# A down projection in seven half-size products over its whole contraction, with block sums added in DRAM

## The chip, the cores and the metric

The kernel runs on one core of one Trainium2 chip. The metric is the device time of one execution, in microseconds (us), lower is better. The core has TensorE (PE, matrix products into the eight banks of PSUM), VectorE (DVE), ScalarE (ACT), GpSimd (POOL) and SyncE (SP); in this kernel SP issues nearly all transfers.

## The reference, cut to what matters

One decoder layer over 1024 tokens of width 1024, all in float32. Everything up to the second residual is the same before and after the change; what counts here is the gated feed-forward part:

```
D_MODEL = 1024;  SEQ = 1024;  D_FF = 2816
x = x + rms_norm(mix, norm_mix_post)
h = rms_norm(x, norm_ffn_pre)
up = causal_dwconv(einsum('bsd,df->bsf', h, ffn_w_up), ffn_conv_w) + ffn_conv_b
gate, val = split(up, 2, axis=-1)
ff = einsum('bsf,fd->bsd', silu(gate) * val, ffn_w_down)      # the down projection
x = x + rms_norm(ff, norm_ffn_post)
```

Ahead of it stand an RMSNorm, the input projection `w_in`, the three mixers (pool, conv, windowed attention) and the output projection `w_o`.

## The kernel before

**How a product is made.** Every float32 operand is split into a rounded part (`hi`, ACT makes it by a copy to the short type) and the rest (`lo`, DVE makes it by subtraction), and each product is three matmuls: hi by hi, lo by hi, hi by lo (helper `product`, lines 1441 to 1443). The unit of PE's work is one matmul of 128 by 128 weights against 512 columns.

**Stages in order.** Input projection and mixers; `w_o` in eight token tiles (ACT squares, POOL computes the root in `root`, lines 563 and 566, DVE scales); the up projection; the down projection with the last norm. The up projection goes over 22 pairs of 128-channel tiles (a gate tile and a value tile). Pairs 0 to 2 are plain (`plain_step`), pairs 3 to 21 use seven products of half size instead of eight (`seventh`, 84 matmuls a pair). For those, POOL adds weight blocks (`sum_weights`, lines 595 to 602), and DVE and ACT split them (`low_entry`, `round_entry`). The gated result of a pair, silu(gate) times value, is made by DVE in `gate_value` (line 1284) in one of two SBUF buffers `yv`; SP writes it to `act_dram` (`save_act`, line 432), since it doesn't fit in SBUF. ACT may write a `yv` buffer again for pair p+2 in `keep`, once the save of pair p has landed (`act_saved`).

**The down projection.** It runs in two passes over the token halves. In each pass the eight banks hold 4 token tiles by 2 output halves, and the 22 channel tiles k run through them: for each k, one weight tile of 128 by 1024 (512 KB, into one of `RAW` = 4 buffers `wraw`) and one activation tile of 128 by 512 (256 KB, `act_in`) are loaded by SP, rounded by ACT (`down_step`), split by DVE (lines 992 and 1269), and used by PE in 24 matmuls (`down_ring`). Two split slots exist. The first two activation tiles are loaded early into `gain_a` (`act_first`). Between the passes ACT and DVE copy the eight banks to `ff`; the first four token tiles are normed and written out in the second pass. The last `TAIL` = 4 channel tiles of the second pass are kept back in buffers of their own, so that the last banks finish one by one: 2 passes x 22 x 24 = 1056 matmuls.

**What sets the order.** Each engine's program is a list in its own order, and semaphores join them; an engine that waits holds everything behind it. POOL in particular does its adds, its roots and its transfers in one list.

## Time and profile before

| what | value |
|---|---|
| time before, median of 3 runs | 1002.41 us (999.76 to 1004.15) |
| profiled execution: time, span | 1003.03 us, 1001.2 us |
| PE busy | 983.2 us (98%), 4580 matmuls |
| DVE, ACT, POOL busy | 613.3 us (61%), 407.8 us, 158.2 us |
| granted TensorE clock, mean | 0.994 |
| bytes moved | 104.90 MB, mean 105 GB/s |

The span is the profiled time from the first to the last instruction; the execution's own time holds 1.83 us more. A busy PE is not PE at its peak: its matmul records are pipelined and overlap (each is 0.39 us long, and they start 0.23 us apart), so that distances between starts are read, not lengths.

### The profile page before, as it was taken

How to read it: one execution, taken by the hardware profiler on the slowest of the kernel's cores; microseconds unless marked ns; L12 is line 12 of the kernel's file. 1: busy time of each engine (PE TensorE's matmuls, PEld its weight loads, DVE VectorE, ACT ScalarE, POOL GpSimd, SP SyncE). 2: the span in 40 equal slices, each digit the busy share in tenths (PEclk: the TensorE clock that was granted, in tenths of full speed). 3: DMA queues.
4: the chain of work that ended last, by engine and by line, in shares of the span. 5: the costliest groups of instructions: out<-in, count | busy, mean ns of one | idle time of the engine just before them, and what ended most of it. 6: DMA issues, size and time to landing. Idle time of an engine off the chain costs nothing.

```text
span 1001.2 us, 11938 instructions
## 1 busy us (share of the span) xinstructions
PE 983.2 (98%) x4580; PEld 810.0 (81%) x4580; DVE 613.3 (61%) x641; ACT 407.8 (41%) x624; POOL 158.2 (16%) x143
## 2 busy tenths in 40 slices
PE   8999999999999998999999999999999999999997
PEld 7988777777888887888888888888887888888886
DVE  4646786664555579777677677677665333344454
ACT  5525444443343335444445445445433323333342
POOL 2200000000111832332242232232200000000001
PEclk9999999999999999999999999999999999999999
DMA  6511110016223321232223223223315444455553
GB/s 221 154 49 37 43 43 22 25 61 209 85 85 104 86 84 47 80 93 86 75 79 90 84 66 102 85 64 105 105 64 191 155 139 144 157 191 197 182 175 126
DMA packets 84911, 104.90 MB, mean 105 GB/s; under 512 B 3849, under 2 KB 63489, under 8 KB 84865
## 3 DMA queue, kind: packets, MB, share of 16 engines
q1 hardware_dynamic: 84737, 104.20, 31.9%
q8 instruction: 31, 0.51, 0.2%
q14 instruction: 15, 0.12, 0.0%
q0 software_dynamic: 128, 0.07, 0.0%
HBM read 84.33 MB, written 19.92 MB: 104 GB/s over the span
## 4 chain that ended last, share of the span: by engine, by line
PE 91%; DVE 3%; DMA 2%; ACT 1%; POOL 1%; issue 1%; SPq 0%; DVEq 0%; POOLq 0%; ACTq 0%
PE ps L1441 29%; PE ps L1442 29%; PE ps L1443 29%; PE ps L1451 1%; PE ps L1549 1%; PE ps L1572 1%; DMA wraw<-in_w_in 1%; PE ps L1550 1%; PE ps L1558 1%; PE ps L1576 1%; DMA wraw<-in_w_o 1%; DMA act_in<-act_dram 0%; DVE hlo L992 0%; PE ps L1587 0%; DVE w2lo L1316 0%
## 5 line engine op out<-in xcount | busy, mean ns | idle before, releaser
L992 DVE TENSOR_TENSOR wlo<-wraw,whi 128x1024 fp32r<-128x1024 f32 x60 | 75.8, 1265 | 138.1 <-ACT whi L633 137.8
L633 ACT ACTIVATE whi<-wraw 128x1024 fp32r<-128x1024 f32 x60 | 63.4, 1058 | 173.4 <-PE ps L1443 169.3
L1441 PE MATMUL ps<-whi,ahi 128*128 128x512 f32 x320 | 124.6, 389 | 1.6 <-DVE alo L1269 1.6
L1443 PE MATMUL ps<-whi,alo 128*128 128x512 f32 x320 | 124.5, 389 | 0.0
L1442 PE MATMUL ps<-wlo,ahi 128*128 128x512 f32 x320 | 124.5, 389 | 0.0
L1441 PE MATMUL ps<-hhi,whi 128*128 128x512 f32 (+1 forms) x256 | 96.4, 376 | 2.3 <-DVE hlo L1010 2.3
L1442 PE MATMUL ps<-hlo,whi 128*128 128x512 f32 (+1 forms) x256 | 93.7, 366 | 0.0
L1443 PE MATMUL ps<-hhi,wlo 128*128 128x512 f32 (+1 forms) x256 | 93.7, 366 | 0.0
L563 POOL TENSOR_SCALAR meansq<-sumsq 128x1 f32<-128x1 f32 x28 | 7.6, 272 | 526.7 <-ACT x2b L804 241.7
L595 POOL TENSOR_TENSOR w_sums<-wraw 128x1024 f32<-128x1024 f32 x19 | 46.7, 2459 | 255.2 <-DVE h2lo L1316 103.4
L1441 PEld LDWEIGHTS ps<-whi,ahi 128*128 128x128 f32 x320 | 60.1, 188 | 14.4 <-DVE alo L1269 2.0
L1443 PEld LDWEIGHTS ps<-whi,alo 128*128 128x128 f32 x320 | 60.1, 188 | 12.6
L1442 PEld LDWEIGHTS ps<-wlo,ahi 128*128 128x128 f32 x320 | 60.1, 188 | 12.4
L1441 PE MATMUL ps<-h2hi,whi 128*128 128x512 f32 x168 | 65.5, 390 | 0.0
L1442 PE MATMUL ps<-h2lo,whi 128*128 128x512 f32 x168 | 65.4, 389 | 0.0
L1443 PE MATMUL ps<-h2hi,wlo 128*128 128x512 f32 x168 | 65.4, 389 | 0.0
L1441 PEld LDWEIGHTS ps<-hhi,whi 128*128 128x128 f32 x256 | 49.1, 192 | 10.0 <-DVE hlo L1010 2.7
L1443 PEld LDWEIGHTS ps<-hhi,wlo 128*128 128x128 f32 x256 | 49.1, 192 | 7.6
L1442 PEld LDWEIGHTS ps<-hlo,whi 128*128 128x128 f32 x256 | 49.1, 192 | 7.4 <-issue 0.5
L1441 PE MATMUL ps<-hhi,mhi 128*128 128x512 f32 x128 | 51.3, 401 | 2.2 <-DVE hlo L992 2.2
L1442 PE MATMUL ps<-hlo,mhi 128*128 128x512 f32 x128 | 50.6, 395 | 0.0
L1443 PE MATMUL ps<-hhi,mlo 128*128 128x512 f32 x128 | 50.5, 394 | 0.0
(196 smaller groups left out, 2215.8 us busy)
## 6 DMA issues: line engine op xcount, KB each, us to landing
wraw<-in_ffn_w_up SPq DMA_DIRECT2D x44, 512.0 KB, 5.1
wraw<-in_ffn_w_down SPq DMA_DIRECT2D x44, 512.0 KB, 3.4
act_dram<-yv SPq DMA_DIRECT2D x22, 512.0 KB, 2.6
act_in<-act_dram SPq DMA_DIRECT2D x42, 256.0 KB, 3.5
wraw<-in_w_in SPq DMA_DIRECT2D x14, 512.0 KB, 4.0
xin<-in_x SPq DMA_DIRECT2D x8, 512.0 KB, 4.3
wraw<-in_w_o SPq DMA_DIRECT2D x8, 512.0 KB, 3.3
xres<-in_x SPq DMA_DIRECT2D x8, 512.0 KB, 4.2
```

Of the source, the lines that this page charges most:

```text
L595: pool.tensor_tensor(w_sums[:, 0:2, :], raw[:, 0:4:3, :], raw[:, 2:3, :].broadcast_to([P, 2, HALF]), ALU.add)\
L633: act.activation(hi[:, slot, :], wraw[:, base % RAW, :], ACT.Copy)\
L992: dve.tensor_tensor(lo[:, slot, :], wraw[:, base % RAW, :], hi[:, slot, :], ALU.subtract).then_inc(w_split, 1)
L1441: pe.matmul(acc, w_hi, x_hi, start=first, stop=False, skip_group_check=looped)
L1442: pe.matmul(acc, w_hi, x_lo, start=False, stop=False, skip_group_check=looped)
L1443: return pe.matmul(acc, w_lo, x_hi, start=False, stop=last, skip_group_check=looped)
L1451: last = pe.transpose(ps[:, b + k // 4, (k % 4) * P:(k % 4 + 1) * P], rows[:, k * P:(k + 1) * P], ident)
L1549: pe.matmul(acc, q, k_hi[:, kv, keys], start=True, stop=False)
L1550: last = pe.matmul(acc, q, k_lo[:, kv, keys], start=False, stop=True)
L1558: last = pe.transpose(ps[:, 6, i * P:(i + 1) * P], prob[:, u % 2, i, :], ident)
L1572: last = pe.matmul(acc, v_tok[:, b, cols], pt_cur[:, heads, :].rearrange("p h q -> p (h q)"), start=True, stop=b == 0)
L1576: last = pe.matmul(acc, v_tok[:, b - 1, cols], pt_prev[:, heads, :].rearrange("p h q -> p (h q)"), start=False, stop=True)
```

## The change

The down projection is no longer two passes of eight blocks. The contraction (2816 channels) is cut in two halves of `HK` = 11 channel tiles (near and far), the tokens in two halves of 512, the output columns in two halves of 512. With A[channel half][token half] the activations and W[channel half][column half] the weights, seven products of 11 channel tiles each are made (the numbers are those of `DOWN_PRODUCTS`, in the order in which they run):

- 1: A11 by W11; 2: A21 by W21; 7: (A22 - A12) by s3; 5: (A11 - A12) by s1; 6: (A11 - A12 + A22) by s2; 3: A22 (negated in the split) by s4; 4: (A11 - A12 + A22 - A21) by W22,
- with s1 = W12 + W22, s3 = W11 + W12, s2 = W11 + s1, s4 = W21 + s2.

Each product has 11 steps of 12 matmuls (4 token tiles x 3): 924 matmuls. A step loads two tiles of 128 by 512 (256 KB each) side by side in one `wraw` buffer, and they are split as one 128 by 1024 tile, in one of six slots (`DOWN_RING`). The first two steps of a product run tile by tile, so do its last two (the last four of the last product), which gives ACT and DVE time to copy or add the finished banks (`copy_product`, `add_product`) before PE takes them again.

The sums are not made by an engine. The weight sums s1 to s4 are made in DRAM: POOL issues four copies of 1408 by 512 blocks (2.88 MB each), waits for them, and issues adding transfers (`accum_op`) onto them, in the stretch in which it had nothing to do (after its three memsets, ahead of the roots of the `w_o` stage); the last of them it issues after the quarter sums. The activation combinations go into `r_dram`: for pairs below 11, SP writes the blocks (five transfers of 256 KB instead of one of 512 KB), for pairs 11 to 21 POOL issues three adding transfers of 256 KB (`add_act`) between its weight sums. DVE makes the difference of the two token halves for each pair (`act_sum`, 128 by 512) in `gate_value`. ACT's rewriting of `yv` now also waits for the adding transfers (`buffer_saved`).

The core of the diff:

```
+HK = NF // 2
+DOWN_PRODUCTS = ((1, 0, True), (2, 0, False), (7, 4, True), (5, 0, True), (6, 0, False),
+                 (3, 0, False), (4, 4, False))
+STEPS = 7 * HK
+DOWN_RING = 6
+LEAD = 2
...
+            def load_step(s):
+                i, k = divmod(s, HK)
+                if s < RAW:
+                    sp.wait_ge(u_split, 4 * (SEVEN - 2 + s // 2) + 4)
                 else:
+                    sp.wait_ge(d_split, s - RAW + 1)
...
+                sp.dma_start(wraw[:, raw, 0:HALF], act_src).then_inc(down_landed[raw], 16)
+                sp.dma_start(wraw[:, raw, HALF:], w_src).then_inc(down_landed[raw], 16)
...
+                if p < HK:
+                    sp.dma_start(act_dram[rows, 0:HALF], yv[:, j, 0:HALF]).then_inc(act_saved[j], 16)
+                    sp.dma_start(r_dram[7][rows, :], yv[:, j, HALF:]).then_inc(act_saved[j], 16)
+                    sp.wait_ge(sum_ready, p + 1)
+                    for i in (5, 6, 4):
+                        sp.dma_start(r_dram[i][rows, :], act_sum).then_inc(sum_saved, 16)
...
             pool.wait_ge(ht_split, NT)
             for buf in (pool_u, sum_a, sum_b):
                 pool.memset(buf[:, 0:PAD], 0.0).then_inc(pads, 1)
+            for i, (d, k) in ((1, (1, 0)), (3, (0, 0)), (2, (0, 0)), (4, (0, 1))):
+                pool.dma_start(s_dram[i][:, :], w_down_blocks[d, k]).then_inc(w_copied, 16)
+            pool.wait_ge(w_copied, 16 * 4)
+            pool.dma_start(s_dram[1][:, :], w_down_blocks[1, 1], accum_op=ALU.add)\
+                .then_inc(w_summed, 16)
+            pool.dma_start(s_dram[3][:, :], w_down_blocks[1, 0], accum_op=ALU.add)\
+                .then_inc(w_summed, 16)
+            pool.wait_ge(w_summed, 32)
+            pool.dma_start(s_dram[2][:, :], s_dram[1][:, :], accum_op=ALU.add,
+                           max_dma_last_dim=4 * HALF).then_inc(w_summed, 16)
             for i in range(NT, 3 * NT):
                 root(i, i + 1)
...
+            def add_act(p):
...
+                pool.wait_ge(act_ready, p + 1)
+                pool.wait_ge(act_saved[k % 2], saved(k))
+                pool.wait_ge(sum_saved, 48 * (k + 1))
+                for i in (7, 6):
+                    pool.dma_start(r_dram[i][rows, :], yv[:, j, HALF:], accum_op=ALU.add)\
+                        .then_inc(act_added[j], 16)
+                pool.wait_ge(sum_ready, p + 1)
+                pool.dma_start(r_dram[4][rows, :], act_sum, accum_op=ALU.add).then_inc(sum_added, 16)
...
+                dve.wait_ge(act_ready, p + 1)
+                if p >= 1:
+                    sum_saved_of(dve, p - 1)
+                dve.tensor_tensor(act_sum, y[:, far], y[:, near],
+                                  ALU.add if p < HK else ALU.subtract).then_inc(sum_ready, 1)
...
+            for s in range(4, STEPS):
+                i, k = divmod(s, HK)
+                if k == LEAD and i - 1 in (2, 4, 5):
+                    for t in range(4):
+                        add_product(i - 1, t)
+                low_step(s)
+                if i == 6 and LEAD + 2 <= k < LEAD + 6:
+                    finish_tile(k - LEAD - 2)
...
+            for i, (_, bank, fresh) in enumerate(DOWN_PRODUCTS):
+                at_end = LEAD if i < 6 else TAIL
+                groups = [range(LEAD)] + [range(k, k + 1) for k in range(LEAD, HK - at_end)]
+                groups.append(range(HK - at_end, HK))
+                for ks in groups:
                     for t in range(4):
...
+                            if t == 0:
+                                pe.wait_ge(d_split, s + 1)
+                            hi, lo = step_place(s, False), step_place(s, True)
+                            last = product(ps[:, bank + t, :], hi[:, tok], lo[:, tok], hi[:, HALF:],
+                                           lo[:, HALF:], fresh and k == 0, k == HK - 1, True)
```

POOL's list around the three memsets, before the change:

```order
27 L574 DMA pool_mat<-in_pool_w 64x64 x3
28 L578 MEMSET pool_u 128x16 [waits ht_split]
29 L578 MEMSET sum_a 128x16
30 L578 MEMSET sum_b 128x16
31 L563 TENSOR_SCALAR meansq<-sumsq 128x1 [waits squares_summed]
32 L566 TENSOR_TENSOR rstd<-meansq,power 128x1 [waits meansq_ready]
```

The same place after it:

```order
28 L610 MEMSET pool_u 128x16 [waits ht_split]
29 L610 MEMSET sum_a 128x16
30 L610 MEMSET sum_b 128x16
31 L613 DMA s_dram<-in_ffn_w_down 1408x512 x4
32 L615 DMA s_dram<-in_ffn_w_down 1408x512 [waits down_weight_blocks_copied]
33 L617 DMA s_dram<-in_ffn_w_down 1408x512
34 L620 DMA s_dram<-s_dram 1408x512 [waits down_weight_blocks_added]
35 L595 TENSOR_SCALAR meansq<-sumsq 128x1 [waits squares_summed]
36 L598 TENSOR_TENSOR rstd<-meansq,power 128x1 [waits meansq_ready]
```

Seven transfers and two waits on transfers now stand ahead of the roots of the `w_o` stage.

DVE's list in the second pass of the down projection before (one norm of a 1024-wide tile and the splits of one channel tile after it):

```order
549 L1392 SCALAR_TENSOR_TENSOR ob<-ff,rstd,gain_a 128x1024
550 L985 REGISTER_ALU
551 L1394 ISA [waits dve_step]
552 L1395 TENSOR_TENSOR ob<-ob,x2f 128x1024 [waits x2_in0]
553 L991 REGISTER_ALU
554 L992 TENSOR_TENSOR wlo<-wraw,whi 128x1024 [waits w_rounded]
555 L1268 REGISTER_ALU
556 L1269 TENSOR_TENSOR alo<-act_in,ahi 128x512 [waits act_rounded]
```

DVE's list in the last of the seven products after (the line 1338 is one step's split, 1471 the adding of a finished bank, 1476 and 1480 the norm of one token tile):

```order
612 L1471 TENSOR_TENSOR ffb<-ps,ffb 128x512 [waits down_banks_done] x4
613 L1338 TENSOR_TENSOR w2lo<-wraw,w2hi 128x1024 [waits down_steps_rounded] x2
614 L1338 TENSOR_TENSOR dlo<-wraw,dhi 128x1024 [waits down_steps_rounded]
615 L1476 SCALAR_TENSOR_TENSOR ob<-ffb,rstd,gain_a 128x1024 [waits rstd_ready]
616 L1480 TENSOR_TENSOR ob<-ob,x2f 128x1024 [waits x2_in0,dve_step]
617 L1338 TENSOR_TENSOR dlo<-wraw,dhi 128x1024 [waits down_steps_rounded]
618 L1476 SCALAR_TENSOR_TENSOR ob<-ffb,rstd,gain_a 128x1024 [waits rstd_ready]
619 L1480 TENSOR_TENSOR ob<-ob,x2f 128x1024 [waits x2_in1,dve_step]
```

The four norms, which stood one in every four channel tiles, now stand behind four steps in a row, each of them half as long for PE.

## Rows read from the trace of the kernel before

**Rows 1.** The page: busy by engine; clock; chain; a group (busy, mean ns | idle).

```profile
PE 983.2 (98%) x4580; PEld 810.0 (81%) x4580; DVE 613.3 (61%) x641; ACT 407.8 (41%) x624; POOL 158.2 (16%) x143
...
PEclk9999999999999999999999999999999999999999
...
PE 91%; DVE 3%; DMA 2%; ACT 1%; POOL 1%; issue 1%; SPq 0%; DVEq 0%; POOLq 0%; ACTq 0%
...
L633 ACT ACTIVATE whi<-wraw 128x1024 fp32r<-128x1024 f32 x60 | 63.4, 1058 | 173.4 <-PE ps L1443 169.3
```

**Rows 2.** Timeline of PE: start, length, instruction, idle time before it with its releaser.

```profile
753.83 0.39 PE L1441 MATMUL ps<-whi,ahi 128*128 128x512 f32 x1
...
764.48 0.39 PE L1443 MATMUL ps<-whi,alo 128*128 128x512 f32 x1
766.49 0.50 PE L1441 MATMUL ps<-whi,ahi 128*128 128x512 f32 x1 [1.62 <-DVE alo L1269]
```

**Rows 3.** Timeline of DVE in the first pass, two channel tiles.

```profile
838.64 1.23 DVE L992 TENSOR_TENSOR wlo<-wraw,whi 128x1024 fp32r<-128x1024 f32 x1 [3.61 <-ACT whi L633]
...
844.08 1.23 DVE L992 TENSOR_TENSOR wlo<-wraw,whi 128x1024 fp32r<-128x1024 f32 x1 [3.61 <-ACT whi L633]
```

**Rows 4.** Timeline of POOL: its idle stretch ahead of the `w_o` stage.

```profile
34.14 2.29 POOL L574 DMA_DIRECT2D pool_mat<-in_pool_w  x4
...
39.40 0.11 POOL L578 MEMSET sum_b<- 128x16 f32 x1
237.08 0.18 POOL L563 TENSOR_SCALAR meansq<-sumsq 128x1 f32<-128x1 f32 x1 [197.57 <-ACT x2b L804]
```

**Rows 5.** DMA issues: KB each, median us to landing.

```profile
wraw<-in_ffn_w_down SPq DMA_DIRECT2D x44, 512.0 KB, 3.4
...
act_in<-act_dram SPq DMA_DIRECT2D x42, 256.0 KB, 3.5
wraw<-in_w_in SPq DMA_DIRECT2D x14, 512.0 KB, 4.0
```

**Rows 6.** Windows: busy us of each engine (x instructions), granted clock, DMA share, GB/s.

```profile
764.00:768.00 4.00, 2.38 (x11) 1.62 (x10) 2.59 (x4) 2.10 (x3) 0.00 (x0) 1.00 1.01 349
...
885.00:905.00 20.00, 20.00 (x90) 16.57 (x89) 8.90 (x9) 6.83 (x9) 0.00 (x0) 1.00 0.59 209
```

**Rows 7.** The chain in order of time, around the step from plain to seven-product pairs.

```profile
391.32 2.28 DVE r_lo L1301
```

**Rows 8.** Timelines of DVE, ACT and POOL in one pair of the steady up stage.

```profile
604.85 1.28 DVE L1264 SCALAR_TENSOR_TENSOR yv<-ps,par_a,yv 128x1022 f32<-128x1022 f32 x1
606.17 1.23 DVE L1284 SCALAR_TENSOR_TENSOR yv<-yv,yg 128x1024 f32<-128x1024 f32 x1
...
609.87 0.60 ACT L877 ACTIVATE yv<-ps 128x512 f32<-128x512 f32 x1 [2.12 <-PE ps L1443]
...
628.91 0.60 ACT L877 ACTIVATE yv<-ps 128x512 f32<-128x512 f32 x1 [2.12 <-PE ps L1443]
...
611.45 1.23 DVE L1316 TENSOR_TENSOR w2lo<-w_sums,w2hi 128x1024 fp32r<-128x1024 f32 x1 [2.92 <-ACT w2hi L864]
...
615.08 2.39 POOL L595 TENSOR_TENSOR w_sums<-wraw 128x1024 f32<-128x1024 f32 x1 [13.57 <-DVE h2lo L1316]
```

**Rows 9.** Timeline of DVE: one norm in the second pass.

```profile
884.91 1.28 DVE L1392 SCALAR_TENSOR_TENSOR ob<-ff,rstd,gain_a 128x1024 f32<-128x1024 f32 x1 [0.84 <-POOL rstd L566]
886.34 1.23 DVE L1395 TENSOR_TENSOR ob<-ob,x2f 128x1024 f32<-128x1024 f32 x1
887.61 1.23 DVE L992 TENSOR_TENSOR wlo<-wraw,whi 128x1024 fp32r<-128x1024 f32 x1
```

**Rows 10.** Timelines of ACT and DVE: the last bank.

```profile
995.31 0.60 ACT L972 ACTIVATE yg<-ps 128x512 f32<-128x512 f32 x1 [2.03 <-PE ps L1443]
...
996.03 0.69 DVE L1424 TENSOR_TENSOR ob<-ps,gain_a 128x512 f32<-128x512 f32 x1 [2.03 <-ACT yg L972]
...
997.27 1.41 DVE L1431 SCALAR_TENSOR_TENSOR ob<-ob,rstd,x2f 128x512 f32<-128x512 f32 x2 [0.55 <-POOL rstd L623]
```

More of the change, by code:

```diff
@@ L348, in build, with saved, added, buffer_saved @@
         score_view = banks(4).rearrange("p (i w j) -> p i w j", w=2, j=P)
-        NQ = 6
+        def saved(p):
+            return 16 * sum(2 if i < HK else 1 for i in range(p % 2, p + 1, 2))
+        def added(p):
+            return 32 * len(range(HK + (HK + p) % 2, p + 1, 2))
+        def buffer_saved(engine, p):
+            engine.wait_ge(act_saved[p % 2], saved(p))
+            if p >= HK:
+                engine.wait_ge(act_added[p % 2], added(p))
+        def sum_saved_of(engine, p):
+            if p < HK:
+                engine.wait_ge(sum_saved, 48 * (p + 1))
+            else:
+                engine.wait_ge(sum_added, 16 * (p + 1 - HK))
+        def step_place(s, lo):
+            at = s % DOWN_RING
+            return (((wlo if lo else whi), (w2lo if lo else w2hi), (dlo if lo else dhi))[at // 2])[:, at % 2, :]
+        def step_raw(s):
+            return (DOWN0 + s) % RAW
         def block_of(hi, i):
@@ L892, in start_value, with round_step, copy_product, square @@
                    .then_inc(yv_started, 1)
-            def round_act(raw, hi, slot):
-                act.activation(hi[:, slot, :], raw, ACT.Copy).then_inc(a_rounded, 1)
+            def round_step(s):
+                i = s // HK
+                before = s - DOWN_RING
+                if s < 2:
+                    act.wait_ge(seven_done, 7 * (SEVEN - 2) + 6 + s)
+                elif s < 4:
+                    act.wait_ge(seven_done, 7 * (SEVEN - 1) + 2 + s)
+                elif s < DOWN_RING:
+                    act.wait_ge(seven_done, 7 * SEVEN)
+                elif before % HK >= HK - LEAD:
+                    act.wait_ge(bank_done, 4 * (before // HK + 1))
+                else:
+                    act.wait_ge(step_done, (HK - LEAD) * (before // HK) + before % HK + 1)
+                act.wait_ge(down_landed[step_raw(s)], 32 * (s // RAW + 1))
+                hi, raw = step_place(s, False), wraw[:, step_raw(s), :]
+                if i == NEGATED:
+                    act.activation(hi[:, 0:HALF], raw[:, 0:HALF], ACT.Copy, scale=-1.0)
+                    act.activation(hi[:, HALF:], raw[:, HALF:], ACT.Copy).then_inc(d_rounded, 1)
+                else:
+                    act.activation(hi, raw, ACT.Copy).then_inc(d_rounded, 1)
+            def copy_product(i, t):
+                out = {0: ffb[:, t, 0:HALF], 1: ffa[:, t, 0:HALF], 3: ffa[:, t, HALF:]}[i]
+                act.wait_ge(bank_done, 4 * i + t + 1)
+                act.activation(out, ps[:, t, :], ACT.Copy).then_inc(part_copied, 1)
+            def square(src, total, seen):
+                if seen > 0:
+                    act.wait_ge(squared, 3 * NT + seen)
+                act.activation(src[1], src[0], ACT.Square, accum_out=total).then_inc(squared, 1)
             for q in x2_saved:
@@ L977, in _ @@
+            for t in range(4):
+                square((ffa[:, t, 0:HALF], yg[:, 0, 0:HALF]), half_sums[:, 2 * t:2 * t + 1], 4 + t)
+            for t in range(4):
+                act.wait_ge(bank_done, 24 + t + 1)
+                square((ps[:, 4 + t, :], yg[:, 0, 0:HALF]), half_sums[:, 2 * t + 1:2 * t + 2], 8 + t)
         @block.vector
@@ L1398, in _ @@
             dve.wait_ge(gain_out_in, 16)
-            dve.wait_ge(ff_act, 2)
-            dve.wait_ge(ff_dve, 2)
-            start = steps[0]
-            with dve.Fori(0, 4) as it:
-                steps[0] = start + it
-                for j in range(4):
-                    down_step(d1 + 2 + j, it, a1 + 2 + j)
-                    if j == 0:
-                        finish(ff[:, bass.ds(it, 1), :].rearrange("p o c -> p (o c)"),
-                               3 * NT, 3 * NT + 1 + it, 0, 16 * it + 16)
-                dve.wait_ge(out_saved[0], 16 * it + 16)
@@ L1426, in _ @@
[L1426 to L1432 removed]
+                    dve.scalar_tensor_tensor(ob[:, t, cols], ob[:, t, cols],
+                                             rstd[:, i:i + 1], x2f[:, t, cols],
@@ L1703, in _ @@
                 seventh(q, 7, 3, 0, r_hi[3], r_lo[3], v0, False)
-            def down_ring(t, k, first=False, last_k=False):
-                tok, slot = slice(t * P, (t + 1) * P), k % 2
-                for c in range(2):
-                    cols = slice(c * HALF, (c + 1) * HALF)
-                    last = product(ps[:, 2 * t + c, :], ahi[:, slot, tok], alo[:, slot, tok],
-                                   whi[:, slot, cols], wlo[:, slot, cols], first, last_k, True)
-                return last
```

414 lines of the change are left out of this document (183 added, 231 removed).

## The prediction, made before the changed kernel ran

> **What bounds the kernel now.** I read the page first. PE is busy for 98% of the span, and the chain that ended last lies on PE for 91% [rows 1]; the granted clock stands at 9 tenths or more in every slice, so nothing is to be had from the clock. Then PE's timeline at the start of the down projection, for the distance between starts, since the lengths overlap. From 753.83 to 764.48 us there are 48 matmuls, so 10.65 / 47 = 0.2266 us each [rows 2]. DVE's rows say the same from the other side: one channel tile of 24 matmuls takes 844.08 - 838.64 = 5.44 us, 0.2267 us each [rows 3], and in each DVE waits 3.61 us for ACT, which waits for PE. So in the down projection PE sets the pace and the others wait for it. There is one gap, before the activation tiles of the first pass arrive: the next start is 766.49, 2.01 us after the last, which is 1.78 us too late [rows 2]. DMA isn't the limit either: while PE ran without a gap from 885 to 905 us, 209 GB/s were moved at a share of 0.59, and in a burst 349 GB/s [rows 6].
>
> **The change, part by part.**
>
> *Products.* 1056 matmuls become 7 x 11 x 12 = 924, of the same form (128 by 128 weights, 512 columns). 132 x 0.2267 = **-29.9 us**, on the path. The order of the loops can't make a matmul shorter, and if the feed keeps up not longer.
>
> *The gap at 764.5 us.* It came from activations that could be loaded only after the last pair was saved. Now products 1 and 2 begin with the near and the far channels of the first token half; the steps up to 10 read only pairs 0 to 10, saved long before. Next late at this place would be DVE: it ends the last pair about 8 us after the up projection's last matmul (two taps each for gate and value, 1.28 us apiece, the product 1.23 [rows 8] and the new difference 0.7), while four steps, 4 x 2.72 = 10.9 us of PE work, are split beforehand. **-1.8 us.** It could come back as 0 to 2 us if step 4 is late.
>
> *Weight sums in DRAM.* Seven transfers on POOL. Their cover is the stretch from 39.40 to 237.08 us in which POOL waits 197.57 us [rows 4]. Ahead of the roots POOL waits for four copies (11.5 MB written) and two additions (5.8 MB). No row shows a transfer from DRAM to DRAM, or one that adds. From below: at 349 GB/s [rows 6] 17.3 MB take 50 us. From above: at the rate of one lone load of `w_in`, 512 KB in 4.0 us = 131 GB/s [rows 5], and twice that time for the additions, 88 + 88 = 176 us, and if the loads of `w_in` and `w_o` in the stretch (18 tiles of 512 KB, 72 us at the same rate) take their turns in full, 248 us, 50 us too many. Issuing: POOL spends 2.29 / 4 = 0.57 us on a transfer of 64 rows [rows 4]; if that goes by rows, 1408 rows are 12.6 us, six of them 75 us, beside the moving. I take **0 us**, near the lower end, since sixteen engines with a long list in front of them look like the burst and not like the lone load; the ends are 0 and +50. The w_in loads are held back by sharing, but each has four buffers' lead (over 30 us), so I give that 0 (at most +2). The fourth sum is issued after the quarter sums and is needed 57 us into the down projection: 0.
> The Trainium skill says under "Collectives: The Full Stack" (The bandwidth ceiling: the fold count and why AG ≠ RS ≠ AR) that an adding transfer reads two sources and so moves at half the speed of a copy; by that the additions cost what two copies do, an estimate that lies inside my bounds and leaves the term at 0.
> A rule against this change is in "SBUF — State Buffer" (Summary: rules for kernel authors): transfers issued by GpSimd wait for descriptors while VectorE is in one of its fast copy modes. DVE's subtraction of 128 by 1024 takes 1.23 us here [rows 3], about one element per lane and cycle of the 0.96 GHz which the skill's first page (Trainium Kernel Development and Optimization, NeuronCore Architecture) gives, so by the rule nothing would starve; no row shows such a transfer beside DVE.
>
> *Activation sums.* Per pair DVE gets one more 128 by 512 operation, 0.69 us as in [rows 10], and a wait for its own result, some 0.85 us in all. In the steady pairs DVE idles 2.92 us right behind it [rows 8]: hidden. Once it isn't: after pair 2 the chain runs through DVE (split of r at 391.32) [rows 7]: **+0.85 us** (0 to +2). POOL's three adding transfers per pair cost 3 x 0.57 to 3 x 1.15 us of issue, in a stretch of 13.57 us idle [rows 8]: hidden. ACT rewrites a `yv` buffer in `keep`, at 609.87 and 628.91 [rows 8]. The result of pair p is ready at 606.17 + 1.23 = 607.4, and the rewriting of its buffer comes one pair after the next `keep`, at 628.91: 21.5 us for issue and landing of transfers of 256 KB, of which plain ones land in 3.5 us [rows 5]. 0 us; each microsecond by which they overrun the 21.5 would cost 11 us, one per pair from 11 on.
>
> *Feeding the steps.* A step moves 512 KB in 2.72 us, 193 GB/s; 209 were carried without a gap [rows 6]. ACT (1.06 us [rows 1]) and DVE (1.23 [rows 3]) need less than 2.72 each, and four raw buffers allow 4 x 2.72 - 1.06 - 1.23 = 8.6 us per load, against 3.4 to 3.5 us [rows 5]. 0 us; if the loads bound the steps at x us each, 77 x (x - 2.72).
>
> *Six changes of product.* PE comes back to a bank 4.1 us after it left it (three other tiles of 6 matmuls), and a copy or an addition of 128 by 512 is 0.7 us. ACT and DVE take up step 2 of the next product only after the last bank: 0.7 + 1.06 + 1.23 = 3.0 us, and PE has two steps, 5.44 us. 0 us (at most +1 each).
>
> *Last product.* After its step 4, DVE does a norm of 2.70 us (884.91 to 887.61 [rows 9]) behind each of four splits of 1.15: 3.85 us for each step against PE's 2.72. Counted from the end of the sixth product, DVE has added its last bank at 0.9 us, begins the split of step 4 at 3.6 (ACT, which also squares the finished rows, is the later one there), those of steps 5 to 8 at 3.85 us each after the last (7.45, 11.3, 15.15, 19.0), and ends that of step 10 at 19.0 + 3 x 1.15 = 22.5. PE runs steps 0 to 6 until 19.04; its last four steps go tile by tile, three matmuls each, so it wants step 10 at 21.0: **+1.5 us** (0 to +3.5). DVE's four small products follow (2.4 us), and the last banks then come every 2.72 us to a DVE that needs 2.65 for each (0.69 and 1.41 and the wait for the root, 0.55 [rows 10]), and catches up little: **+0.5 us** (0 to +2). The rest of the end, from the last bank's square at 995.31 to the last row of DVE and its store [rows 10], stays.
>
> *Sum.* -29.9 - 1.8 + 0 + 0.85 + 0 + 0 + 1.5 + 0.5 = -28.85 us. The span of 1001.2 becomes 972.3, the execution 1003.03 - 28.85 = 974.2 us; it lay 0.6 us above the median, so on the median's footing 973.6. I predict **974 us**.
>
> **Rivals.**
> *POOL held by the weight sums: slower.* If the six transfers last longer than the 197.57 us, the roots of the `w_o` stage are late by the rest, and PE with them. It decides against the change from a delay of 28 us on, that is, below 17.3 MB / 226 us = 77 GB/s. At 60 GB/s they last 288 us: +90 us, 1065 us. For it: no row shows such transfers, and two waits in a list do stand there. Against it: even the pessimistic rate leaves a tie.
> *The steps are fed too slowly: same or a little slower.* Two loads of half the size per step, from blocks in DRAM with a pitch of their own; a step of 3.1 us (169 GB/s) eats the whole gain, 1003 us; 3.2 us gives 1012. Against it: 209 GB/s ran without a gap.
> *A part of the gain is lost in waits: 985 to 997 us.* The adding transfers overrun their 21.5 us by 1 or 2 us (+11 to +22), or each change of product costs 2 us (+12).
> *The change doesn't do what it says:* matmul starts 0.2267 us apart would have to grow; with the same form I see no reason.
>
> **How the numbers follow.** Forecast (970 to 985): 0.70. Part of the gain lost (985 to 997): 0.13. Fed too slowly (997 to 1015): 0.06, half of it within the band of no change. POOL held (1007 to 1100): 0.09. Matmuls slower: 0.02, slower than before. A measurement of this kernel can tell about 0.5% (5 us) from no change. Faster by more: 0.70 + 0.13 = 0.83; within: 0.04, with some of the others' edges; slower: 0.13. The range leaves out 2 in 10 at most: from 969 (without the costs of the last product, 972, and a little) to 995.
>
> **What would show it right or wrong.** Right: 924 matmuls of the down projection at 0.227 us; POOL's first root of the `w_o` stage still near 237 us; no gap of PE near 764 us; a gap of about 2 us in the last 15 us, with DVE's split of step 10 as its releaser; in the up stage ACT's `keep` never released by a transfer. Wrong: a first root after 240 us released by a DMA; gaps of PE behind `wraw` loads, at steps or at changes of product; starts further apart than 0.23 us; a longer idle time of PE near 395 us than one more microsecond.

## The result, and the profile after

The changed kernel took 972.7 us (median of 4 runs, 971.0 to 973.7) against 1001.6 us for the kernel before beside it (median of 4, 999.8 to 1004.2): a ratio of 0.9705, 95% interval 0.9689 to 0.972. The prediction was 974 us, within 969 to 995. The profiled execution took 972.8 us with a span of 971.0; the profiled span before was 1001.2, so 30.2 us are to be found. I first show where they are, then the experiments.

The page of the kernel after, answering to [rows 1] and [rows 5]: busy time by engine, the clock in 40 slices, the chain that ended last, and DMA issues with KB each and median us to landing.

```profile
PE 951.6 (98%) x4448; PEld 783.6 (81%) x4448; DVE 651.4 (67%) x688; ACT 424.9 (44%) x634; POOL 197.9 (20%) x184
...
PEclk9999999999999999899999999999999999999999
...
PE 90%; DVE 5%; DMA 3%; ACT 1%; issue 0%; SPq 0%; POOL 0%; DVEq 0%; POOLq 0%; ACTq 0%
...
s_dram<-in_ffn_w_down POOLq DMA_DIRECT2D x6, 2816.0 KB, 28.2
...
wraw<-in_w_in SPq DMA_DIRECT2D x14, 512.0 KB, 11.0
```

PE has 4580 - 4448 = 132 matmuls fewer. It still bounds the kernel, busy for 98% of the span. DVE has risen from 613.3 to 651.4 us and from 3% to 5% of the chain. The one low slice of the clock is the 17th, at 388 to 413 us.

PE's timeline after: start, length, instruction, and the idle time before it with its releaser. First the gap between the plain pairs and the first seven-product pair, then the start of the down projection, the place of the old gap [rows 2], and the last matmul.

```profile
391.12 0.39 PE L1515 MATMUL ps<-r_hi,w2lo 128*128 128x512 f32 x1
395.52 0.76 PE L1513 MATMUL ps<-r_hi,h2hi 128*128 128x512 f32 x1 [4.01 <-DVE h2lo L1397]
...
754.45 0.39 PE L1513 MATMUL ps<-whi 128*128 128x512 f32 x1
...
764.42 0.39 PE L1515 MATMUL ps<-w2hi,w2lo 128*128 128x512 f32 x1
764.65 0.39 PE L1513 MATMUL ps<-w2hi 128*128 128x512 f32 x1
...
963.71 0.39 PE L1515 MATMUL ps<-dhi,dlo 128*128 128x512 f32 x1
```

Three distances make up the whole difference (those of before: first and last matmul of the down projection at 753.83 and 994.88).

| | before, us | after, us | difference | forecast |
|---|---|---|---|---|
| start of the span to first matmul of the down projection | 753.83 | 754.45 | +0.62 | +0.85 |
| from there to the start of its last matmul | 241.05 | 209.26 | -31.79 | -30.2 |
| from there to the end of the span | 6.32 | 7.29 | +0.97 | +0.5 |

The first row is within what executions of one order differ by: in five more traces of kernels that are the same up to there, the down projection starts between 752.68 and 756.28 us. The middle row is worth a calculation. 924 matmuls have 923 distances, and 923 x 0.2267 = 209.2 us; 209.26 were measured. Through 77 steps and six changes of product PE doesn't wait once. The two matmuls at 764.42 and 764.65 stand 0.23 us apart where [rows 2] had 2.01.

### The profile page after: what moved, and what is told of

Its sections match the earlier page's. It is cut to its first block, busy times and chain, and to the rows that moved or that the text cites. A ratio compares the mean times of both kernels' runs of the same rounds, so it can differ in the third digit from the quotient of the medians.

```text
span 971.0 us, 11470 instructions
## 1 busy us (share of the span) xinstructions
PE 951.6 (98%) x4448; PEld 783.6 (81%) x4448; DVE 651.4 (67%) x688; ACT 424.9 (44%) x634; POOL 197.9 (20%) x184
## 3 DMA queue, kind: packets, MB, share of 16 engines
q0 software_dynamic: 13456, 31.79, 16.4%
## 4 chain that ended last, share of the span: by engine, by line
PE 90%; DVE 5%; DMA 3%; ACT 1%; issue 0%; SPq 0%; POOL 0%; DVEq 0%; POOLq 0%; ACTq 0%
PE ps L1513 28%; PE ps L1514 28%; PE ps L1515 28%; DMA r_dram<-cst 1%; PE ps L1523 1%; PE ps L1621 1%; DMA xin<-in_x 1%; PE ps L1644 1%; PE ps L1622 1%; PE ps L1630 1%; DVE r_lo L1382 1%; DMA wraw<-in_w_o 1%; PE ps L1648 1%; DVE yv L1357 0%; DVE hlo L1054 0%
## 5 line engine op out<-in xcount | busy, mean ns | idle before, releaser
L949 ACT ACTIVATE yg<-ps,par_b 128x1024 f32<-128x1024 f32 x19 | 22.9, 1207 | 55.4 <-DVE ps L1407 55.4
L1513 PE MATMUL ps<-r_hi,h2hi 128*128 128x512 f32 x104 | 41.5, 399 | 4.0 <-DVE h2lo L1397 4.0
L1324 DVE SCALAR_TENSOR_TENSOR yg<-ps,par_a,yg 128x1023 f32<-128x1023 f32 x22 | 28.2, 1282 | 25.4 <-ACT yg L949 25.4
L1338 DVE TENSOR_TENSOR wlo<-wraw,whi 128x1024 fp32r<-128x1024 f32 x23 | 27.8, 1223 | 25.1 <-ACT whi L979 24.8
L1514 PE MATMUL ps<-r_lo,h2hi 128*128 128x512 f32 x104 | 41.4, 398 | 0.0
L1515 PE MATMUL ps<-r_hi,h2lo 128*128 128x512 f32 x104 | 41.3, 397 | 0.0
L1513 PE MATMUL ps<-r_hi,w2hi 128*128 128x512 f32 x104 | 40.5, 390 | 0.0
L1515 PE MATMUL ps<-r_hi,w2lo 128*128 128x512 f32 x104 | 40.5, 389 | 0.0
```

Of the source, the lines that this page charges most:

```text
L949: act.activation(yg[:, pair % 2, :], banks(4 * (pair % 2)), ACT.Identity, bias=ffn_bias(pair), scale=ffn_tap(2, pair)).then_inc(yg_started, 1)
L1324: finish_step(dve.scalar_tensor_tensor(y[:, 1:], src[:, :SEQ - 1], ffn_tap(1, f), y[:, 1:], ALU.mult, ALU.add))
L1338: dve.tensor_tensor(lo, raw, hi, ALU.subtract).then_inc(d_split, 1)
L1513: pe.matmul(acc, w_hi, x_hi, start=first, stop=False, skip_group_check=looped)
L1514: pe.matmul(acc, w_hi, x_lo, start=False, stop=False, skip_group_check=looped)
L1515: return pe.matmul(acc, w_lo, x_hi, start=False, stop=last, skip_group_check=looped)
```

## The experiments

Each starts from the changed kernel and makes one edit, unless the text says otherwise.

### Copies in DRAM, made three and five times

The largest risk was POOL, which issues the weight sums and waits for them ahead of the roots of the `w_o` stage. POOL's timeline after, answering to [rows 4]:

```profile
39.00 3.46 POOL L613 DMA_DIRECT2D s_dram<-in_ffn_w_down  x4
83.85 1.55 POOL L615 DMA_DIRECT2D s_dram<-in_ffn_w_down  x1 [41.39 <-DMA s_dram<-in_ffn_w_down]
84.74 2.17 POOL L617 DMA_DIRECT2D s_dram<-in_ffn_w_down  x1
122.30 1.47 POOL L620 DMA_DIRECT2D s_dram<-s_dram  x1 [35.38 <-DMA s_dram<-in_ffn_w_down]
237.88 0.18 POOL L595 TENSOR_SCALAR meansq<-sumsq 128x1 f32<-128x1 f32 x1 [114.11 <-ACT x2b L868]
```

Four copies of 2816 KB, 11.53 MB, are written from 39.00 to 83.85: 257 GB/s. Two additions, 5.77 MB, take until 122.30: 38.45 us, 150 GB/s. Both ran beside the loads of `w_in`. One transfer of 1408 rows costs POOL 3.46 / 4 = 0.87 us of issue, so that doesn't go by rows. Then POOL still waits 114.11 us, for ACT. So about 83 of the 197.57 us of cover in [rows 4] were used. The Trainium skill says under "Collectives: The Full Stack" (The bandwidth ceiling: the fold count and why AG ≠ RS ≠ AR), of a ReduceScatter in a ring of cores, that its add needs two source reads where a copy needs one, and so reaches about half the bandwidth. Here the ratio was 257 / 150 = 1.7, with loads running beside both.

To see whether the cover is what counts, the copies were repeated:

```diff
-            pool.wait_ge(w_copied, 16 * 4)
+            for again in range(2):          # 4 in the second kernel
+                pool.wait_ge(w_copied, 64 * (again + 1))
+                for i, (d, k) in ((1, (1, 0)), (3, (0, 0)), (2, (0, 0)), (4, (0, 1))):
+                    pool.dma_start(s_dram[i][:, :], w_down_blocks[d, k]).then_inc(w_copied, 16)
+            pool.wait_ge(w_copied, 64 * 3)  # 64 * 5 in the second
```

> The changed kernel with its four weight copies done three times in a row (each round waits for the one before), then the additions as before. In the changed kernel POOL's list went 39.0 (issue), 83.9 (copies landed), 122.3 (two additions landed), and its next root began at 237.9 us. Theory 1 (the transfers have a cover of POOL's idle time, and cost nothing until it is used up): the additions land near 39 + 3 x 42 + 38 = 203 us, before 237.9, so the time stays at 972.7 us within 2 us. Theory 2 (the transfers already cost time by holding back the loads of w_in, which land in 17.8 us instead of 4.0 beside them): twice as long beside them costs time, 5 us or more. PE's first gap after 40 us tells: at 231 us by theory 1, earlier by theory 2.

> The same with the four copies done five times. Theory 1 (a cover of 114 us is left, and beyond it the roots of the w_o stage are late by the rest): the additions land at 39 + 45 + 4 x 40 to 45 + 38 = 282 to 302 us, the first root is late by 45 to 64 us, and the time is 1018 to 1037 us; PE has one gap of that length. Theory 2 (what counts is the sharing of the DMA engines with w_in and w_o loads): the loss would be spread over many gaps ahead of 230 us.

Measured: 976.0 us (2 runs; ratio 0.9738, interval 0.971 to 0.9766) and 1036.5 us (2 runs; 1.0342, 1.0275 to 1.041). In the first, POOL's timeline has the third addition at 212.52, and the root only 3.4 us later than after, with ACT as its releaser:

```profile
212.52 1.47 POOL L624 DMA_DIRECT2D s_dram<-s_dram  x1 [33.36 <-DMA s_dram<-in_ffn_w_down]
241.27 0.18 POOL L595 TENSOR_SCALAR meansq<-sumsq 128x1 f32<-128x1 f32 x1 [27.28 <-ACT x2b L872]
```

In the second, the timelines of POOL and PE show the root right behind the third addition, and PE standing still:

```profile
303.30 1.48 POOL L624 DMA_DIRECT2D s_dram<-s_dram  x1 [29.94 <-DMA s_dram<-in_ffn_w_down]
304.85 0.18 POOL L595 TENSOR_SCALAR meansq<-sumsq 128x1 f32<-128x1 f32 x1
...
311.88 1.51 PE L1527 MATMUL ps<-cst,hrow_c 128*128 128x128 f32 x6 [60.24 <-DVE hrow_c L1320]
```

The root is 304.85 - 237.88 = 67 us late, and the time 64 us longer. So the forecast's slower rival is a real mechanism, with the price and place it was given; the change stands about 114 us away from it. The first kernel is 3.3 us slower than 972.7 and 1.4 slower than 974.6, the changed kernel's second measurement (below), so its time is near theory 1 and not at the 5 us of theory 2. What its trace shows beyond the changed kernel's is something else: its DMA engines were still full when the loads of `w_o` came (they landed in 9.0 us, 3.9 after, medians of four from 200 to 240 us), and PE had four gaps of 1.2 to 2.2 us at 227 to 238 us.

### Twice the feed

```diff
                 sp.dma_start(wraw[:, raw, HALF:], w_src).then_inc(down_landed[raw], 16)
+                if s >= 12:
+                    n = (s - 12) // 4
+                    if n:
+                        sp.wait_ge(spare_in[s % 4], 16 * n)
+                    sp.dma_start(spare[:, s % 4, :], w_down[near, :]).then_inc(spare_in[s % 4], 16)
```

> The changed kernel with one more load of 512 KB per step from step 12 on, into a spare buffer that nobody reads: 1 MB instead of 512 KB per step, 386 GB/s at a step of 2.72 us. Theory 1 (the steps are fed with room to spare up to the DMA engines' rate, of which the traces show 349 GB/s over 4 us): the feed becomes the bound, 1.05 MB / 349 = 3.0 us per step, 65 x 0.28 = +18 us, 985 to 1000 us. Theory 2 (the steps are limited by the latency of a load and have little room already at 193 GB/s): loads land much later, over 10 us, and the time passes 1003 us. Theory 3 (even this is hidden): 973 us.

Measured: 979.9 us (2 runs; ratio 0.9778, 0.9748 to 0.9807), 7 us more than after (5 more than its second measurement, 974.6). Windows of that kernel (busy us of PE, PEld, DVE, ACT, POOL with instructions, granted clock, DMA share, GB/s):

```profile
800.00:840.00 40.00, 40.00 (x179) 33.10 (x178) 16.98 (x14) 16.37 (x18) 0.00 (x0) 1.00 1.01 386
...
850.00:900.00 50.00, 50.00 (x222) 41.44 (x221) 23.99 (x30) 22.45 (x34) 0.00 (x0) 1.00 1.04 397
```

The change itself moves 206 GB/s at a share of 0.61 from 780 to 940 us. With almost twice that, PE still ran without a gap in the 40 and 50 us of these rows. From its first to its last matmul of the down projection it lost 6.0 us: 1.7 at 844 us, 0.4 twice near 910 and 2.8 from 956 to 961, behind splits or sums that came late, and the rest in slower starts. Behind the last matmul the span goes on for 9.93 us instead of 7.29, since DVE's small products wait 5.15 us for the stores of `ob`. The time lies between theory 3 (973) and theory 1 (985 to 1000). So the feed has a margin of nearly two in the middle of the stage, and a price where something else comes on top (the reload of `x2f`, 2 MB; the stores at the end). The rival "fed too slowly" is out.

### Two of the three matmuls of each product

The third matmul of each product of the down projection (its high half by the other's low half) is left out: 616 instead of 924, so a step takes PE 1.81 us and asks for 289 GB/s.

```diff
-                            last = product(ps[:, bank + t, :], hi[:, tok], lo[:, tok], hi[:, HALF:],
-                                           lo[:, HALF:], fresh and k == 0, k == HK - 1, True)
+                            last = two_products(ps[:, bank + t, :], hi[:, tok], lo[:, tok],
+                                                hi[:, HALF:], lo[:, HALF:], fresh and k == 0,
+                                                k == HK - 1)
```

> The changed kernel without the third matmul (hi by lo) of every product of the down projection, so that part of the sum is left out: 616 matmuls instead of 924, everything else the same. Theory 1 (PE sets the pace of the down projection at 0.2267 us per matmul, and loads, ACT and DVE follow): 308 x 0.2267 = 69.8 us less, of which the last product gives some back, since DVE's norms of 2.5 us and a split of 1.15 stand against steps of 1.81 us (about 7 us more): 903 to 915 us. Theory 2 (the feed is close behind: loads land in 3.4 to 4.5 us, and with rounding and splitting 6.6 us are spread over four buffers, 1.65 us per step, or the loads share 289 GB/s badly): a step takes 2.2 us or more, 77 x 0.4 = 30 us come back, 933 us or more.

Measured: 937.1 us (2 runs; ratio 0.935, 0.9309 to 0.9392), which is in the range of theory 2, though not by steps that are all longer: the loss has places. 308 matmuls less are 69.8 us of PE; 35.6 came out. The distance from first to last matmul is 171.49 us where 615 x 0.2267 = 139.4 would do. The 32.1 us: 13.4 in seven gaps of over 0.46 us up to 900 us (of them 5.8 at one place), 11.7 after 900, in the last product, and the rest small waits and matmuls at the lower clock. The timelines of SP, ACT and PE at the largest:

```profile
811.11 1.95 SPq L571 DMA_DIRECT2D x2f<-x_dram  x4
...
822.11 1.06 ACT L979 ACTIVATE dhi<-wraw 128x1024 fp32r<-128x1024 f32 x1 [6.41 <-DMA wraw<-s_dram]
...
818.48 0.39 PE L1512 MATMUL ps<-w2hi,w2lo 128*128 128x512 f32 x1
824.48 0.80 PE L1511 MATMUL ps<-dhi 128*128 128x512 f32 x1 [5.61 <-DVE dlo L1338]
```

Four loads of `x2f`, 2 MB, stand in SP's list ahead of the steps' loads; ACT waits 6.41 us for a load behind them, and PE gets its step 5.8 us late. At PE's full work the same burst costs nothing (209.26 us above). So in the changed kernel PE alone sets the pace of the stage, but at some places with little to spare. With a third of the matmuls gone, half of what they cost PE was lost again, a third of that loss in the last product. I conclude, without a run, that a further cut of products would need the reload and the norms moved first.

### The norms of the last product, made longer

The norm's first operation is done a second time.

```diff
+                finish_step(dve.scalar_tensor_tensor(ob[:, t, :], ffb[:, t, :],
+                                                   rstd[:, 3 * NT + t:3 * NT + t + 1],
+                                                   gain_a[:, :], ALU.mult, ALU.mult))
                 dve.wait_ge(x2_in[t], 16)
```

> The changed kernel with the first operation of each of the four norms in the last product done twice (1.3 us more each, 5.2 us in all, on DVE only). In the changed kernel DVE ended the split of step 10 at 954.90 and PE's first matmul of it started at 955.10, so there is 0.2 us of room. Theory 1 (the last product's norms are just hidden, with no room left): PE gets a gap of 4.5 to 5.2 us before step 8 to 10, and the time rises by 4 to 6 us to about 978 us. Theory 2 (there is more room than these starts show, since PE runs tile by tile): less than 2 us.

Measured: 978.1 us (4 runs; ratio 0.9753, 0.9723 to 0.9784), 3.5 and 5.4 us more than the two medians of the changed kernel (974.6 and 972.7); the profiled span is 4.5 longer. PE's timeline of that kernel:

```profile
951.97 0.40 PE L1518 MATMUL ps<-whi,wlo 128*128 128x512 f32 x1
956.31 0.80 PE L1516 MATMUL ps<-w2hi 128*128 128x512 f32 x1 [3.95 <-DVE w2lo L1338]
```

The gap is the one that theory 1 gave. So DVE's chain through four norms and the splits of steps 4 to 10 is what PE meets next, and in the changed kernel it ends just in time. DVE's timeline after, answering to [rows 9]:

```profile
937.04 1.22 DVE L1338 TENSOR_TENSOR dlo<-wraw,dhi 128x1024 fp32r<-128x1024 f32 x1
938.18 1.28 DVE L1476 SCALAR_TENSOR_TENSOR ob<-ffb,rstd,gain_a 128x1024 f32<-128x1024 f32 x1
...
940.64 1.22 DVE L1338 TENSOR_TENSOR dlo<-wraw,dhi 128x1024 fp32r<-128x1024 f32 x1
...
953.68 1.22 DVE L1338 TENSOR_TENSOR dlo<-wraw,dhi 128x1024 fp32r<-128x1024 f32 x1
```

A norm takes 940.64 - 938.18 = 2.46 us, not the 2.70 of [rows 9], and split and norm together 3.60, not 3.85. The split of step 10 ends at 953.68 + 1.22 = 954.90, and PE starts on step 10 at 955.05.

### The gap at 391 us: the token difference later

The releaser of PE at 395.52 is DVE's `h2lo`, which comes after pair 2's products, the new difference and a split of `r`. The difference for that pair was moved behind three more splits, so that it stands in nobody's way:

```diff
             low_difference(2)
             low_entry(0, 2)
             low_entry(0, 3)
             low_difference(3)
+            token_difference(PLAIN - 1)
```

> The changed kernel with DVE's difference of the token halves of pair 2 moved behind the four splits that follow it. Theory 1 (this one operation stands on the chain before PE's gap at 391 us): the split that ends the gap comes 0.6 us earlier, PE's gap shrinks from 4.17 to about 3.5 us, and the time by 0.6 to 1.2 us (the matmuls after the gap start 0.43 us apart instead of 0.23 for a while, and that stretch may be shorter too). Theory 2 (the gap is set by the waits of ACT): no change of the gap.

Measured: 971.4 us (4 runs; ratio 0.9683, 0.9657 to 0.9708), not to be told from after. The timelines of PE and ACT of that kernel:

```profile
389.62 0.39 PE L1522 MATMUL ps<-r_hi,w2lo 128*128 128x512 f32 x1
394.00 0.76 PE L1520 MATMUL ps<-r_hi,h2hi 128*128 128x512 f32 x1 [3.99 <-ACT yg L943]
...
393.32 1.06 ACT L943 ACTIVATE yg<-ps 128x512 f32<-128x512 f32 x2
```

The gap is 4.38 us, and 4.40 after. In seven more traces of kernels with the order unaltered here it is 4.40 to 5.00, so a gain of some tenths can't be excluded; the 0.6 us and more of theory 1 didn't come. Its releaser is now ACT's copy of the first product, which ACT does behind its own roundings; in the kernel before, the gap of 3.73 us (391.32 to 395.05) had the same releaser. Two engines are late here by nearly the same, and moving work off one of them buys next to nothing.

### The end, with a buffer of its own

The timelines of DVE and ACT after, at the end, answering to [rows 10]:

```profile
957.05 0.69 DVE L1493 TENSOR_TENSOR ob<-ffa,gain_a 128x512 f32<-128x512 f32 x1 [0.94 <-DMA out<-ob]
959.55 0.69 DVE L1493 TENSOR_TENSOR ob<-ffa,gain_a 128x512 f32<-128x512 f32 x1 [1.81 <-DMA out<-ob]
...
964.13 0.60 ACT L990 ACTIVATE yg<-ps 128x512 f32<-128x512 f32 x1 [2.03 <-PE ps L1515]
...
966.32 0.68 DVE L1497 SCALAR_TENSOR_TENSOR ob<-ps,gain_a 128x512 f32<-128x512 f32 x1
967.04 1.41 DVE L1503 SCALAR_TENSOR_TENSOR ob<-ob,rstd,x2f 128x512 f32<-128x512 f32 x2
```

The small products write to `ob`, whose rows of the first half are still being stored, and wait 2.75 us for the stores. DVE is then busy without a pause and takes the last bank 966.32 - 964.13 (ACT's square of it) = 2.2 us after ACT; before, it was 0.72 us [rows 10]. The edit lets them write to `ffb`, in all places where `ob` stood, and drops the wait:

```diff
-                dve.wait_ge(out_saved[t], 16)
-                dve.tensor_tensor(ob[:, t, 0:HALF], ffa
+                dve.tensor_tensor(ffb[:, t, 0:HALF], ffa
```

> The changed kernel with the last four token tiles finished in the buffer ffb instead of ob, so that DVE needs no longer wait until the first four results are stored. In the changed kernel DVE waited 0.94 and 1.81 us for those stores (which took 7.4 us to land beside reloads of x2), and its work on the last bank began 2.3 us after ACT's square of it, against 0.7 before. Theory 1 (the longer end comes from that wait): the time from PE's last matmul to the end of the span falls from 7.3 to 6.3 us, 1.0 us less in all. Theory 2 (it comes from DVE needing 2.05 to 2.7 us for each bank that comes every 2.72 us): no change.

Measured: 969.9 us (4 runs; ratio 0.9668, 0.9643 to 0.9693), against 972.7 and 974.6 (below) for the changed kernel; the intervals overlap, so the times alone don't settle it, and the trace is sharper. DVE's timeline of it:

```profile
954.83 2.49 DVE L1492 TENSOR_TENSOR ffb<-ffa,gain_a 128x512 f32<-128x512 f32 x4
...
964.89 0.69 DVE L1496 SCALAR_TENSOR_TENSOR ffb<-ps,gain_a 128x512 f32<-128x512 f32 x1
```

The four small products now run in one piece. The last matmul starts at 963.74 there and the span ends at 970.1: 6.4 us, where after had 7.29 and before 6.32. In the two later kernels with this edit the end is 6.31 and 6.32 us long; in four others with the shared buffer and PE not held up here, 7.22 to 7.52. About 0.9 us of the end is this wait, the rest of the difference in medians isn't shown by anything at the end.

### Both, with the splits in another order

Both edits were then put together, and around pair 2 ACT's copy of the first product and the roundings, and DVE's splits, were put where PE wants them first (on DVE: `low_entry(0, 2)` ahead of pair 2's value taps and `low_difference(2)` ahead of its products).

> The changed kernel with both of the last edits and a third: ahead of the first seven-product pair, ACT rounds and DVE splits the entry that PE waits for (the third of pair 3) as soon as PE has left its place, before the differences of the activations, and ACT keeps PE's first partial product before it rounds the last difference. Theory 1 (PE's gap at 391 us and the slow matmuls behind it, 0.43 us apart, are both due to the order of ACT's and DVE's work): the gap of 4.2 us goes, the slow stretch with it (11 matmuls x 0.2 = 2.3 us), the end is 1 us shorter: 965 to 968 us. Theory 2 (another wait takes the gap's place, such as the partial product that has to be kept, or the shared port of DVE and POOL): at least 2 us of gap stay, 969 us or more.

Measured: 970.6 us (5 runs; ratio 0.967, 0.9644 to 0.9695). The gap at 391 is gone, and another is there at 402.40 to 406.19, with matmuls 0.43 us apart behind it. At 402.40 PE had started the last matmul of pair 3's sixth product, and its list goes on to the seventh, which waits for the fold of the second partial product (a fold is DVE's adding of a kept partial product to a bank). The profile names no releaser for that gap; the fold ends at 405.40 + 0.68 = 406.08, and PE starts at 406.19. DVE's timeline:

```profile
401.39 1.21 DVE L1410 TENSOR_TENSOR wlo<-wraw,whi 128x1024 fp32r<-128x1024 f32 x1
402.53 1.21 DVE L1410 TENSOR_TENSOR wlo<-w_sums,whi 128x1024 fp32r<-128x1024 f32 x1
403.66 0.68 DVE L1420 TENSOR_TENSOR ps<-ps,yg 128x512 f32<-128x512 f32 x1
404.26 1.21 DVE L1410 TENSOR_TENSOR w2lo<-w_sums,w2hi 128x1024 fp32r<-128x1024 f32 x1
405.40 0.68 DVE L1420 TENSOR_TENSOR ps<-ps,yg 128x512 f32<-128x512 f32 x1
```

Three splits for the next pair, which PE wants one, two and three products (2.7 to 8.2 us) later, stand ahead of the second fold. So theory 2 was right that the gap moves on, but the rows point at the order. Something else had made DVE late too: beside POOL's weight sums its two operations of `gate_value` on 128 by 512 took 1.78 and 1.77 us instead of 0.69 and 0.68. The next kernel changes the order alone (the difference of pair 2 leaves its place ahead of the loop for the one shown):

```diff
-                if q + 1 < SEVEN:
+                if q == 0:
+                    low_entry(1, 0)
+                    fold(0, 0)
+                    fold(0, 1)
+                    low_entry(1, 1)
+                    token_difference(PLAIN - 1)
+                    low_entry(1, 2)
+                    low_entry(1, 3)
+                elif q + 1 < SEVEN:
```

> The kernel before the first seven-product pair reordered as in the kernel with all three edits, and now the two folds of the first such pair stand ahead of three of the four weight splits of the next pair on VectorE, with pair 2's token difference behind them; the end writes to a buffer of its own. Theory 1 (the gap of about 4 us near 391, which the last kernel only moved to 402, is set by the order of VectorE's rows, and so are the slow matmuls that follow it): PE stands at most about 1 us there, the slow rows go too, in all 3.5 + 2 us less than in the kernel with all three edits: 964 to 967 us. Theory 2 (VectorE has more to do here than the time that PE gives it, so that the gap moves on once more, to the start of the next pair): 969 us or more, with a new gap between 405 and 420.

> The changed kernel itself, unaltered, on the same chip as the kernel with the folds moved, so that the two can be held against each other. Both theories: 972.7, within 1.5 us, a gap of about 4.2 us near 391 with slow matmuls behind it.

Measured, both on one chip: 967.6 us (5 runs, 966.5 to 970.2; ratio 0.9661, 0.9638 to 0.9685) and, for the changed kernel unaltered, 974.6 us (5 runs, 972.3 to 974.9; ratio 0.9714, 0.969 to 0.9738). All runs of the one lie below all of the other; the medians are 7.0 us apart. PE's timeline of the kernel with the folds first:

```profile
400.33 0.39 PE L1533 MATMUL ps<-h2hi,h2lo 128*128 128x512 f32 x1
401.24 0.47 PE L1531 MATMUL ps<-r_hi,h2hi 128*128 128x512 f32 x1 [0.52 <-issue]
...
411.73 0.50 PE L1531 MATMUL ps<-r_hi,w2hi 128*128 128x512 f32 x1 [2.05 <-ACT yg L947]
```

What PE lost between 391 and 420 us, gaps and slow matmuls together, was 7.0 us in the unaltered kernel and is 3.1 here; 2.2 of these are a new gap at the start of the next pair, before 411.73. With all three edits and the old place of the folds it was 5.2, so the folds account for some 2 us and the earlier reordering for as much. The two profiled spans differ by 8.1 us: 4.0 from this stretch, 0.9 from the end, 2.4 from the start of the `w_o` stage, and the rest from before it. In those last two stretches the two kernels are alike, and the profiled executions of the other kernels differ there as well (1.3 to 4.3 us lost between 220 and 240 us where the code is the same), so that part isn't the edit's as far as these runs show. The time lies between theory 1 (964 to 967) and theory 2 (969 or more), and each has a part: the gap at the seventh product is down to 0.7 us with DVE's two long operations still there, so the order made most of it, and a smaller gap did move on to where theory 2 put it. This is the fastest kernel here that computes the whole result. Whether the kernel before would gain as much from such an order wasn't tried.

## Why the prediction was right

The sum of the forecast was -28.85 us. The medians differ by 28.9, the profiled spans by 30.2. That the first two agree to a tenth is luck: the last product came out 1.5 us better and the end 0.5 worse than forecast, and the changed kernel measured once more, beside other runs of the kernel before, was 27.6 us faster (974.6 against 1002.2). The mechanism isn't luck: the one large term, fewer matmuls at an unchanged distance, is what was measured. Term by term, by the spans:

- **Products and the old gap.** -29.9 and -1.8 were forecast. 132 matmuls fewer at 0.2267 us, and no gap at 764 us: as forecast, the measured gap of before being worth 1.8 to 1.9. Together they gave 31.8 us, of which the start and the end took 1.6 back.
- **Weight sums.** 0, as taken. The lower bound (349 GB/s for all) was closer than the upper: 83 us. That repeating the copies costs nothing of POOL's until the cover ends, and then all of it, was shown by the two copy kernels. The feared issue by rows (12.6 us) was 0.87.
- **Loads of `w_in`.** 11.0 us to landing, not 4.0 (18.0 for the seven in the stretch of the sums, 39 to 122 us), and no gap of PE from it: 0, as forecast.
- **Activation sums.** +0.85 forecast at pair 2. The gap there grew from 3.73 to 4.40 us (+0.67), and behind it 11 matmuls instead of 8 were slow (+0.8, which the forecast didn't have). A small gap of before at 415.59 (0.6) is gone. With PE 0.2 earlier at the gap, that is +0.62 in all, but by terms that cancel, and the start of the down projection varies by 3.6 us over six traces of the same order. So the term is neither confirmed nor refuted. That the difference's place is the cause of the longer gap is not shown: with it moved, ACT held the gap open to nearly the same length.
- **In the steady pairs** nothing waits for the sums. The timelines of POOL and ACT after, answering to [rows 8]:

```profile
608.32 1.75 POOL L664 DMA_DIRECT2D r_dram<-yv  x2 [6.18 <-DVE yv L1360]
609.44 1.50 POOL L667 DMA_DIRECT2D r_dram<-cst  x1
615.71 2.39 POOL L638 TENSOR_TENSOR w_sums<-wraw 128x1024 f32<-128x1024 f32 x1 [4.76 <-DVE h2lo L1397]
...
629.53 0.60 ACT L943 ACTIVATE yv<-ps 128x512 f32<-128x512 f32 x1 [2.12 <-PE ps L1515]
```

  POOL has 4.76 us left behind the issues (13.57 before), the additions land in 5.8 and 6.9 us (medians from 600 to 640 us), and ACT overwrites the buffer at 629.53, released by PE. The working had one slip that changed nothing: an overrun would have cost nine times its length and not eleven, since the buffers of the last two pairs are not written again.
- **Feeding and changes of product.** 0 each, as forecast; the doubled feed shows the margin. (In the rival's sum a step of 3.2 us gives 1011 us, not 1012.)
- **Last product.** +1.5 was forecast, 0 measured, and the gap near the end that was to show it isn't there: this term failed. The mechanism was right, as the longer norms show, but the term was mis-sized. It took 3.85 us for split and norm from [rows 9] and 3.6 us until the first split; they were 3.60 and about 3.0. Over four steps and the start that is 4 x 0.25 + 0.6 = 1.6 us, all of the term. The norm of [rows 9] runs in a loop before and in straight code after, which may be the 0.24 us; that wasn't tried.
- **End.** +0.5 forecast, +0.97 measured. The forecast looked at DVE's length of work and missed its wait for the stores of `ob`, 2.75 us, of which some 0.9 reach the end.

The range was wide upwards for POOL and the feed; neither came near.

## What to carry to other kernels

A wait in a list costs nothing until its cover is used up and then all of the rest, so measure how much of the cover is left (here 114 us) rather than how long the work takes. When PE stands at a change of stage, look at what its late engine does just before: here splits wanted 2.7 to 8.2 us later stood ahead of a fold wanted at once, and the new orders together gave back 3.9 of the 7.0 us that PE lost there, where moving 0.6 us of work had given next to nothing. When two engines are late together, moving work off one shows nothing.

## What the hardware showed that I had not expected

A gap of PE can cost more than its length. After the 4.40 us at 391.12 the matmuls start 0.43 us apart for 11 of them; windows of the kernel after:

```profile
395.00:400.00 5.00, 4.48 (x11) 3.54 (x12) 5.00 (x3) 0.55 (x2) 4.38 (x2) 0.50 0.56 161
```

The granted clock there is 0.50, so the lower of its levels, 1.2 GHz; it rose again at 400.71. The same stands behind the gap of 2.80 us at 230.90, before's gaps of 2.55 us at 231.13 and 3.73 at 391.32, and the 4.34 us with the longer norms. It doesn't stand behind the 2.01 us of [rows 2], the 2.44 us at 409.29 with the folds first, the 3.32 us at 231.14 with the doubled feed or the 3.71 us at 767.95 with two of three matmuls, so the gap's length alone doesn't tell it. Where it comes it costs 1.5 to 2.9 us, and there the removal of the gap pays about one and a half times.

DVE and POOL were slower beside each other. Of two equal splits of `r` one ran while POOL waited, the next while POOL added weight blocks, from 395.54 on; DVE's timeline after:

```profile
391.95 2.28 DVE L1382 TENSOR_TENSOR r_lo<-r_full,r_hi 128x2048 fp32r<-128x2048 f32 x1
...
395.89 4.45 DVE L1382 TENSOR_TENSOR r_lo<-r_full,r_hi 128x2048 fp32r<-128x2048 f32 x1
```

POOL's addition of 128 by 512 beside it took 3.22 us, and 1.63 in the steady pairs. In the kernel before, the same two splits took 2.28 and 4.45 us as well. No run takes POOL's work away from this place, so what it costs PE is open.

Beside that: copying from DRAM to DRAM went at 257 GB/s and adding at 150, while a core's loads kept landing without a gap on PE; and with all transfers together 386 and 397 GB/s were held for 40 and 50 us.
